# Table E of the state-space stage: four products on VectorE, their sums in pairs on TensorE

## What is computed

```python
dt = exp(log_dt)[:, None]
mag = exp(ar * dt)
lr, li = mag * cos(ai * dt), mag * sin(ai * dt)      # lambda, per group and state
zr, zi = ((lr - 1) * ar + li * ai) / den, (li * ar - (lr - 1) * ai) / den
bbr = zr[..., None] * br - zi[..., None] * bi        # B-bar, complex
bbi = zr[..., None] * bi + zi[..., None] * br
xr = einsum('ntgc,gpc->ntgp', ug, bbr)
xi = einsum('ntgc,gpc->ntgp', ug, bbi)
h[t] = lambda * h[t-1] + x[t]                        # complex, associative scan
y = einsum('ntgp,gcp->ntgc', hr, c_re) - einsum('ntgp,gcp->ntgc', hi, c_im)
```

## Time and profile before

| | |
|---|---|
| median of 3 runs | 2842.31 us (2840.43 to 2843.61) |
| profiled execution | 2846.91 us |
| its span, first to last instruction | 2845.1 us |
| mean granted TensorE clock | 0.97 |
| state-space stage, to the first product of the next phase | 228.94 us |
| TensorE busy over the span | 2688.5 us |
| VectorE busy over the span | 1368.4 us |

### The profile page before, as it was taken

How to read it: one execution, slowest core, us unless ns; L and a number is a source line. 1 busy time by engine, 2 the same in 40 slices (tenths; PEclk the granted TensorE clock), 3 DMA queues, 4 the chain that set the end, 5 groups by cost and what they waited for, 6 DMA issues and landing times.

```text
span 2845.1 us, 44442 instructions
## 1 busy us (share of the span) xinstructions
PE 2688.5 (94%) x18634; PEld 2556.7 (90%) x18634; DVE 1368.4 (48%) x2284; ACT 833.0 (29%) x1682; POOL 269.7 (9%) x435
## 2 busy tenths in 40 slices
PE   5589999999999999999999999888999999999998
PEld 4488999999999999988888888756999999999998
DVE  8972135423332333766667766666254333233325
ACT  7221122111111112335555455443131111111212
POOL 2300000000000000012133424330000000000000
PEclk8689999999999999999999999998999999999999
DMA  3411111111111111322334546466111111111101
GB/s 97 80 36 47 53 37 47 41 46 58 44 43 45 44 44 39 107 69 78 81 78 123 131 114 141 156 216 254 45 45 45 45 44 44 44 44 44 44 30 62
DMA packets 174496, 205.28 MB, mean 72 GB/s; under 512 B 47335, under 2 KB 129687, under 8 KB 174089
## 3 DMA queue, kind: packets, MB, share of 16 engines
q1 hardware_dynamic: 154512, 159.29, 18.5%
q0 software_dynamic: 19840, 44.00, 5.9%
HBM read 156.73 MB, written 27.82 MB: 65 GB/s over the span
## 4 chain that ended last, share of the span: by engine, by line
PE 76%; DVE 8%; ACT 3%; issue 2%; DMA 1%; POOL 1%; SPq 0%; DVEq 0%; ACTq 0%; POOLq 0%
PE PS L221 12%; PE PS L218 11%; PE PS L217 11%; PE PS L396 8%; PE PS L400 8%; PE PS L397 8%; PE PS L2190 4%; PE PS L2191 4%; PE PS L2192 4%; PE PS L2205 2%; PE PS L2232 2%; PE PS L2219 1%; DVE SSB L2121 1%; DVE SQ L191 1%; DVE TMP L328 1%
## 5 line engine op out<-in xcount | busy, mean ns | idle before, releaser
L217 PE MATMUL PS<-XH,WH 128*128 128x352 f32 x1920 | 617.7, 322 | 3.7 <-PEq L103 3.7
L218 PE MATMUL PS<-XL,WH 128*128 128x352 f32 x1920 | 619.0, 323 | 0.0
L396 PE MATMUL PS<-HIDH,WH 128*128 128x352 f32 x1536 | 494.9, 323 | 8.1 <-DVE HIDL L331 8.1
L397 PE MATMUL PS<-HIDL,WH 128*128 128x352 f32 x1536 | 494.6, 323 | 0.0
L221 PE MATMUL PS<-XH,WL 128*128 128x352 f32 x1920 | 414.9, 324 | 0.0
L217 PEld LDWEIGHTS PS<-XH,WH 128*128 128x128 f32 x1920 | 362.4, 189 | 4.2 <-issue 4.1
L218 PEld LDWEIGHTS PS<-XL,WH 128*128 128x128 f32 x1920 | 361.2, 188 | 0.1
L347 DVE TENSOR_TENSOR H<-PS,H 128x1056 f32<-128x1056 f32 x128 | 160.9, 1257 | 391.5 <-PE PS L400 391.1
L400 PE MATMUL PS<-HIDH,WL 128*128 128x352 f32 x1536 | 331.6, 324 | 0.0
L221 PEld LDWEIGHTS PS<-XH,WL 128*128 128x128 f32 x1920 | 329.4, 188 | 0.0
L396 PEld LDWEIGHTS PS<-HIDH,WH 128*128 128x128 f32 x1536 | 289.3, 188 | 12.7 <-DVE HIDL L331 12.7
(11 more groups left out here) (382 smaller groups left out, 3412.2 us busy)
## 6 DMA issues: line engine op xcount, KB each, us to landing
RAW<-w_up SPq DMA_DIRECT2D x32, 1024.0 KB, 5.4
RAW<-w_down SPq DMA_DIRECT2D x32, 1024.0 KB, 4.9
KVR<-cache_kv_w SPq DMA_DIRECT2D x18, 1024.0 KB, 10.5
QB<-QA SPq DMA_DIRECT2D x120, 132.0 KB, 2.5
ARAW<-w_q SPq DMA_DIRECT2D x24, 512.0 KB, 4.8
O_SCRATCH<-OT POOLq DMA_DIRECT2D x96, 128.0 KB, 2.8
OB<-O_SCRATCH POOLq DMA_DIRECT2D x24, 512.0 KB, 6.8
RAW<-w_glu SPq DMA_DIRECT2D x16, 512.0 KB, 4.7
```

Source lines behind the costliest of these rows:

```text
L217: nc.tensor.matmul(out, wh(k), xh[:, k, c], start=(k == 0), stop=False)
L218: nc.tensor.matmul(out, wh(k), xl[:, k, c], start=False, stop=False)
L396: nc.tensor.matmul(out, w, m.hidh[:, k, q], start=(k == 0), stop=False)
L397: nc.tensor.matmul(out, w, m.hidl[:, k, q], start=False, stop=False)
```

## The change

The sum of the two products of each half leaves VectorE. ET holds the four products (two parts for each half), and TensorE adds the two parts of a half into PSUM by two products with the identity in place of one transpose. For the difference VectorE multiplies with the negated imaginary part of B-bar (BBN), made once. ET grows to 16 KB, over PA and PB; W's two scratch tiles move to WA and WB, where JUNK was. VectorE now waits for `et_turned` ahead of a table's first product, and no longer for its own end of a table.

```diff
-        self.et = at("ET", [128, 2, 4, 2, L, GC], F32, H_AT + 4096)
+        self.et = at("ET", [128, 2, 2, 2, 4, L, GC], F32, H_AT + 4096)
+        self.bbn = at("BBN", [128, NQ, GC], F32, WT_AT)
+        self.wa = at("WA", [128, 1024], F32, H_AT + 24576)
+        self.wb = at("WB", [128, 1024], F32, H_AT + 28672)
@@
+        step(nc.vector.tensor_scalar(s.bbn[:], s.bb[:, 1], -1.0, None, ALU.mult))
@@ make_e
-            v = lambda ap: ap[:, 0:512].rearrange("p (n x y) -> p n x y", n=4, x=L)
+            if ch >= 2:
+                dve.wait_ge(f.et_turned, ch - 1)
+            et = s.et[:, ch % 2]
             pwr = [bc(s.pw[:, i, 7::-1, qs].rearrange("p t q -> p q t"), 3, GC) for i in range(2)]
-            bv = [bc(s.bb[:, i, qs, :], 2, L) for i in range(2)]
-            for i, (x, y, op) in enumerate(((0, 1, ALU.subtract), (1, 0, ALU.add))):
-                nc.vector.tensor_tensor(v(s.pa), pwr[0], bv[x], ALU.mult)
-                step(nc.vector.tensor_tensor(v(s.pb), pwr[1], bv[y], ALU.mult))
-                if i == 0 and ch >= 2:
-                    dve.wait_ge(f.et_turned, ch - 1)
-                ins = nc.vector.tensor_tensor(s.et[:, ch % 2, :, i], v(s.pa), v(s.pb), op)
-                if i == 0:
-                    step(ins)
-            ins.then_inc(f.et_ready, 1)
-            dve.wait_ge(f.et_ready, ch + 1)
+            bv = [bc(x[:, qs, :], 2, L) for x in (s.bb[:, 0], s.bb[:, 1], s.bbn)]
+            nc.vector.tensor_tensor(et[:, 0, 0], pwr[0], bv[0], ALU.mult)
+            nc.vector.tensor_tensor(et[:, 0, 1], pwr[1], bv[2], ALU.mult)
+            nc.vector.tensor_tensor(et[:, 1, 0], pwr[0], bv[1], ALU.mult)
+            nc.vector.tensor_tensor(et[:, 1, 1], pwr[1], bv[0], ALU.mult).then_inc(f.et_ready, 1)
@@ table W
-                nc.vector.tensor_tensor(v(s.pa), pv[0], x, ALU.mult)
-                step(nc.vector.tensor_tensor(v(s.pb), pv[1], z, ALU.mult))
-                ins = nc.vector.tensor_tensor(s.w[:, qs, i], v(s.pa), v(s.pb), op)
+                nc.vector.tensor_tensor(v(s.wa), pv[0], x, ALU.mult)
+                step(nc.vector.tensor_tensor(v(s.wb), pv[1], z, ALU.mult))
+                ins = nc.vector.tensor_tensor(s.w[:, qs, i], v(s.wa), v(s.wb), op)
@@ turn_e
-                    mm = tr(ps[:, 6 + q // 2, 256 * (q % 2) + 128 * i:256 * (q % 2) + 128 * i + 128],
-                            s.et[:, ch % 2, q, i].rearrange("p t c -> p (t c)"), m.ident[:])
+                    for part in range(2):
+                        mm = nc.tensor.matmul(ps[:, 6 + q // 2, 256 * (q % 2) + 128 * i:256 * (q % 2) + 128 * i + 128],
+                                              s.et[:, ch % 2, i, part, q].rearrange("p t c -> p (t c)"), m.ident[:],
+                                              start=(part == 0), stop=(part == 1))
```

## The result

The changed kernel takes 2855.59 us (median of 5 runs, 2851.77 to 2857.46) against 2842.31 us before: ratio 1.0040, 95% interval 1.0028 to 1.0052. That is 8 to 15 us slower; the ratio is 11.4 us, the medians lie 13.3 apart. The forecast was 2856.9, slower. The profiled execution took 2855.92 us, span 2854.1.

What follows compares the result with a forecast made beforehand. TensorE and ScalarE's chain turning E and U was taken to set W's start once VectorE is freed. 12.2 + 1.7 + 0.7 = 14.6 us, added to the median 2842.31, gave 2856.9; range 2852 to 2866.

Steps and rivals of the forecast that it cites:

- Where the bound is: State-space stage: the change is worth what it moves W's start; shortening VectorE's chain alone gives nothing.
- E6: Seventh table of E on TensorE, ahead of the last blocks of U: +2.9 us.
- The eight terms: TensorE's chain ahead of W at full clock, tables of E and blocks of U together: 12.2 us.
- E4: Fifth table of E on TensorE, ahead of the sample transposes: 3.9 us for 1.03, +2.9.
- E5: Sixth table of E on TensorE, with U4 to U7: 24 more instructions at 0.122, +2.9 us.
- The clock: TensorE in the second to fourth E tables: mostly full clock, half a burst low, +1.7 us.
- E0: First table of E on TensorE: 7.2 us at half clock, ending near 39.1; costs 0, at most 0.6 us.
- GpSimd: Small operations behind W: more of them run beside GpSimd's arithmetic on the sample states, +0.7 us.
- Rival 1: TensorE's tables: a product is one instruction at 0.12 us, about +1, so 2843 us, not slower; 6%.
- rival 3: TensorE's tables: a product costs four transposes, 7.7 us a table, +37 in all, 2880 us; 2%.
- rival 2: TensorE's clock stays at 1.2 GHz in the second to fourth E tables: 23.7, 2866 us; 13%.
- Shift of W = shift of the end: Behind W: any shift of its start runs on to the end, every later phase keeping its length.

Runs made afterwards that it cites:

- first run: Changed kernel, but TensorE turns only the first part of each half with one transpose, second products left out: 2843.53 us, ratio 0.9998.
- second run: Kernel before, VectorE untouched, with two TensorE products with the identity for each half, the second adding zeros: 2855.39 us, ratio 1.0031.
- fourth run: Kernel before, with the 65 sample transposes and their copies moved behind the last table of E: 2841.56 us, ratio 0.9989.
- third run: Kernel before, with one product with the identity in place of each transpose of E: 2844.96 us, ratio 1.0002.
- fifth run: Changed kernel, with the 65 sample transposes and their copies moved behind the last table of E: 2853.71 us, ratio 1.0034.
- sixth: Kernel before with sample transposes last, first two E tables by products, each quarter of W waiting only for its four U blocks: 2842.58 us, ratio 0.9995.
- seventh: The sixth with the last E table by products as well: 2842.07 us, ratio 0.9997.
- two, small operations moved: The sixth, with the scan's small operations moved from behind W to between the second and third E tables: 2832.21 us, ratio 0.9965.
- three, small operations moved: The seventh, with the scan's small operations moved from behind W to between the second and third E tables: 2837.61 us, ratio 0.9976.
- no products, the same: Kernel before with late sample transposes, quarters of W, small operations between second and third E tables, no products: 2838.66 us, ratio 0.9981.
- changed, small operations moved: Changed kernel, only the scan's small operations moved from behind W to between the second and third E tables: 2846.71 us, ratio 1.0011.

## Why the prediction was right, step by step

- **Where the bound is** held: VectorE's saving was worth nothing (first run), TensorE's part alone gave the whole loss within the intervals (second run), and the shift of W's start arrived whole at the next phase (10.44 and 10.46). The reading behind it, two chains that end within 0.2 us of each other, was not right: with most of its waits for TensorE gone VectorE's chain ended 3.7 us earlier (fourth run). The forecast doesn't hang on that, since either way TensorE's part was the one to price.
- **Two instructions for a product**: held, 256 records. **The price** was a little high: E6, from 71.65 to the start of U behind it at 75.23, is 3.58 for 32, 0.112 each instead of 0.122. (The 0.122 divided a record's own time, which overlaps the next, by 16.) The eight terms, foretold as 12.2, came to 10.4: E1 and E2 +0.7 (a start 0.25 earlier taken off) and +1.0, E3 +1.7, U0 to U3 -0.9, E4 +2.6, U4 to E5 +2.5, E6 +2.7, the sample transposes +0.1. W started at 77.25, not near 81.
- **The clock**, +1.7: 0 in the profiled execution, where E1 to E3 ran at 2.4 GHz; 1.6 us for E1 in the second run. E0 took 5.6 us, not 7.2: the clock rose within it (granted 0.79 in 35:36) and stayed up over the gap of 2.50 us ahead of E1. Which of the two an execution draws isn't known from any row here.
- **GpSimd**, +0.7: 0. The scan starts 37.7 us behind W in both kernels, but as two effects that cancel: one of W's operations meets GpSimd's arithmetic instead of three (-0.9), and the small operations behind W take 7.9 us instead of 7.0 (+0.9). So the 0 is luck in part.
- By its own profile the change costs 10.5 us in the stage. The medians lie 13.3 apart, within an interval of 8 to 15; what lies behind the stage took 2614.7 us after and 2616.2 before, so the nearness of 2856.9 to 2855.59 is largely luck: the sum, 14.6, was 4 us too high for the traced pair and 3 for the ratio of the runs (11.4). The base helped too: the 85 executions of the kernel before beside the later runs have a median of 2844.4 on four chips, 2 us above the 2842.31 that the forecast was added to.
- Rival 1 (a product in one instruction) is out by the 256 records, and it and rival 3 (the price of four transposes) by the third run; rival 2 happened in part, in some executions.
- **W's scratch, the negation, the moved wait** at 0: held (the negation took 0.43 us, and TensorE still started E0 when the gains were copied). "Shift of W = shift of the end" was too simple in the other direction. Where W started earlier, its end ran into the clearing of T, which late samples also move later, and all of the gain was gone at the scan: W 5.3 us earlier and the scan 1.4 later than in the changed kernel (fifth run), W 2.3 and 4.3 earlier and the scan 0.5 and 0.2 later than in the kernel before (sixth and seventh). Only the fourth run kept its gain, 3.5 of 3.7.

## What to carry to other kernels

Two chains that end together may be one chain: take an engine's waits for the other out of its timeline first (4.9 us here). Then price the work that is moved on the engine that takes it before counting what the other one saves; here 1.7 us saved on VectorE cost 2.5 to 2.7 on TensorE for each table that had no cover. Count the instructions of a float product in the trace (two, a transpose is one), and give such work only to the places where the engine waits anyway. An early finish is worth something only if what comes behind meets nothing: ask what runs on GpSimd at the new time, and move short copies into a wait that is there.

## What the runs showed of the hardware that had not been expected

Short VectorE copies last until a GpSimd memset beside them ends (up to 7.0 us for one of 0.17). `tensor_tensor` beside GpSimd's own `tensor_tensor` takes 1.63 us instead of 1.23 (128x1024).

The clock behind the scan is what makes two traces hard to compare. All thirteen, in us (clock: that of the products behind the wait for XL):

| kernel | W starts | scan | T's first product | first product with W | next phase | wait for XL | clock |
|---|---|---|---|---|---|---|---|
| before | 66.81 | 104.51 | 145.87 | 170.15 | 228.94 | 2.35 | half |
| changed | 77.25 | 114.96 | 154.97 | 180.61 | 239.40 | 2.36 | half |
| one part left out | 68.82 | 106.52 | 147.82 | 172.16 | 227.59 | 2.37 | full |
| TensorE's part only | 80.76 | 118.47 | 157.77 | 184.12 | 241.17 | 2.36 | half in part |
| one product | 70.37 | 108.07 | 148.99 | 174.61 | 230.01 | 1.46 | full |
| late samples | 63.07 | 101.03 | 139.71 | 166.69 | 224.60 | 2.36 | half in part |
| changed, late samples | 71.92 | 116.32 | 158.15 | 181.98 | 240.76 | 2.38 | half |
| two tables | 64.48 | 105.04 | 145.89 | 170.69 | 229.47 | 2.35 | half |
| three tables | 62.51 | 104.73 | 146.12 | 171.38 | 225.81 | 1.35 | full |
| two, small operations moved | 64.78 | 94.20 | 141.95 | 163.19 | 218.53 | 2.28 | full |
| three, small operations moved | 64.20 | 93.62 | 144.09 | 169.67 | 223.55 | none | full |
| no products, the same | 67.84 | 97.26 | 143.14 | 166.17 | 221.59 | 2.34 | full |
| changed, small operations moved | 78.86 | 108.69 | 155.57 | 178.00 | 232.40 | 1.33 | full |

In the seven traces in which the first product with W waited for the scan, it came 65.6 to 65.7 us behind the scan's start. Behind a wait of TensorE for XL of 2.3 to 2.4 us the next products ran at half the clock, in whole or in part, in six of nine traces and at the full one in three (one part left out; small operations moved; the same without products); behind waits of 1.3 to 1.5 us, or none, it stayed full in all four. No length of a wait decides it by itself: ahead of E1 the clock stayed up over gaps of 2.22 to 2.89 us in five traces and was down behind one of 2.05 (second run) and one of 1.89 (three tables, small operations moved). The next phase came 57.1 to 58.8 us after the first product with W in the six, and 53.9 to 55.4 in the seven: some 3 us that two executions of nearly the same work may differ by. And executions of one kernel spread by 5 to 13 us, and the time goes with the clock: of the 85 executions of the kernel before, the seven with a mean granted clock of 0.974 took 2839.0 to 2840.1 us, the seven with 0.969 or less 2846.5 to 2850.2.
